# Second block of a two-block transformer: merge gate products spread over the turns of attention

## The reference, cut to what matters

```python
def hybrid_layer(x, norm_g, w_in, w_br_a, w_br_b, w_br_c, w_out, cos, sin):
    h = rmsnorm(x, norm_g)
    proj = h @ w_in                          # 1024 x 8388; m_g is its last 3072 columns
    ...
    ya = moba_attention(...)    * silu(a_g)  # 384 wide
    yb = dsa_attention(...)     * silu(b_g)  # 384 wide
    yc = dilated_mixture(...)   * silu(c_g)  # 256 wide
    gates = sigmoid(m_g).reshape(bsz, seq, 3, 1024)
    merged = (gates[:, :, 0] * (ya @ w_br_a) + gates[:, :, 1] * (yb @ w_br_b)
              + gates[:, :, 2] * (yc @ w_br_c))
    return x + merged @ w_out
```

## Time and profile before

| what | us |
|---|---|
| median of 3 runs | 1746.44 (1740.73 to 1748.66) |
| profiled execution, its time | 1738.29 |
| profiled execution, its span | 1736.5 |
| PE busy in the span | 1581.3 (91%) |
| DVE, ACT, POOL busy | 946.2, 650.5, 263.6 |
| mean granted PE clock | 0.954 of full |

### The profile page before, as it was taken

How to read it: one execution, slowest core, us unless ns; L and a number is a source line. 1 busy time by engine, 2 the same in 40 slices (tenths; PEclk the granted TensorE clock), 3 DMA queues, 4 the chain that set the end, 5 groups by cost and what they waited for, 6 DMA issues and landing times.

```text
span 1736.5 us, 23526 instructions
## 1 busy us (share of the span) xinstructions
PE 1581.3 (91%) x9394; PEld 1291.3 (74%) x9394; DVE 946.2 (54%) x1332; ACT 650.5 (37%) x947; POOL 263.6 (15%) x230
## 2 busy tenths in 40 slices
PE   4899979899999999889889996999879989997997
PEld 2774537888888887765679996789569968875996
DVE  2634443644544557624466767788426667863464
ACT  2434341521112114333443334444543444454333
POOL 0214430100000000314300001120430012125000
PEclk8999989999999999899999998999889989988999
DMA  9313781232222222319545555446105545540352
GB/s 352 97 49 122 277 233 50 72 99 98 97 97 97 97 98 73 117 43 325 137 131 191 174 192 164 144 146 195 50 14 182 182 128 177 163 146 1 115 177 98
DMA packets 168672, 234.19 MB, mean 135 GB/s; under 512 B 8929, under 2 KB 116481, under 8 KB 168449
## 3 DMA queue, kind: packets, MB, share of 16 engines
q1 hardware_dynamic: 168576, 232.86, 41.3%
HBM read 231.79 MB, written 1.05 MB: 134 GB/s over the span
## 4 chain that ended last, share of the span: by engine, by line
PE 71%; DVE 8%; ACT 5%; POOL 3%; issue 2%; DMA 1%; DVEq 0%; POOLq 0%; ACTq 0%
PE psum L615 20%; PE psum L617 19%; PE psum L616 19%; PE psum L816 3%; POOL work L1964 2%; PE psum L849 2%; DVE wl L1382 2%; PE psum L632 2%; PE psum L836 2%; PE psum L821 1%; ACT wh L1095 1%; DVE smax L1591 1%; ACT scr L1082 1%; ACT scr L1079 1%; DVE roped L1557 1%
## 5 line engine op out<-in xcount | busy, mean ns | idle before, releaser
L1382 DVE TENSOR_TENSOR wl<-raw,wh 128x2048 fp32r<-128x2048 f32 (+1 forms) x170 | 384.6, 2262 | 332.6 <-ACT wh L1095 180.2
L615 PE MATMUL psum<-hTh,wh 128*128 128x256 f32 (+1 forms) x1376 | 425.2, 309 | 10.6 <-DVE hTl L1453 6.0
L617 PE MATMUL psum<-hTh,wl 128*128 128x256 f32 (+1 forms) x1376 | 423.8, 308 | 0.0
L616 PE MATMUL psum<-hTl,wh 128*128 128x256 f32 (+1 forms) x1376 | 423.8, 308 | 0.0
L615 PEld LDWEIGHTS psum<-hTh,wh 128*128 128x128 f32 x1376 | 263.1, 191 | 26.6 <-issue 4.4
L616 PEld LDWEIGHTS psum<-hTl,wh 128*128 128x128 f32 x1376 | 263.2, 191 | 12.9
L617 PEld LDWEIGHTS psum<-hTh,wl 128*128 128x128 f32 x1376 | 263.1, 191 | 12.5
L1095 ACT ACTIVATE wh<-raw 128x2048 fp32r<-128x2048 f32 (+2 forms) x108 | 202.4, 1874 | 153.4 <-PE psum L617 142.0
L1270 ACT ACTIVATE wh<-raw 128x2048 fp32r<-128x2048 f32 x62 | 118.9, 1917 | 364.5 <-PE psum L617 364.5
L615 PE MATMUL psum<-wh,hTh 128*128 128x512 f32 (+3 forms) x576 | 221.9, 385 | 11.1 <-DVE hTl L1453 6.5
L617 PE MATMUL psum<-wh,hTl 128*128 128x512 f32 (+3 forms) x576 | 219.0, 380 | 0.0
(11 more groups left out here) (141 smaller groups left out, 1798.5 us busy)
## 6 DMA issues: line engine op xcount, KB each, us to landing
raw<-in_w_in SPq DMA_DIRECT2D x54, 1024.0 KB, 4.9
raw<-in_w_ada SPq DMA_DIRECT2D x48, 1024.0 KB, 6.4
raw<-in_w_gate SPq DMA_DIRECT2D x22, 1024.0 KB, 5.1
...
```

The costliest lines, as they stand in the source:

```text
L615: pe.matmul(o, left[0], right[0], start=first, stop=False)
L616: pe.matmul(o, left[0], right[1], start=False, stop=False)
L617: return pe.matmul(o, left[1], right[0], start=False, stop=last)
L1382: dve.tensor_tensor(wl[:, w % SPLIT, 0:m], raw[:, u % RING, 0:m], wh[:, w % SPLIT, 0:m].bitcast(F32), ALU.subtract).then_inc(lo_ready, 1)
```

## The change

The 12 gate units move from merge2 into att2. `HALF_GATES` gives each of PE's 19 turns one or two slots (after logits, after values) with 24 half-products of 24 matmuls, all accumulated in PSUM bank 7. ACT copies each finished unit raw into free SBUF (L1252 of the new kernel) and casts the next weights; the weights' remainder on DVE stands at the end of a step, the gate multiplication at its start. M stands between A and B. The sigmoids come in merge2, in place. A merge round has one weight unit, in the order A, C, B; DVE makes three products, POOL adds the first two, DVE adds the third, ACT makes hi, DVE makes lo in the next round. In merge2 PE waits for the attention outputs branch by branch.

The diff, cut to its core:

```diff
@@ -71,6 +71,9 @@
+HALF_GATES = [(1, 1) if i in (7, 8, 9, 10, 11) else (0, 1) if i == 18 else (1, 0) for i in range(19)]
+GATES_BY = [sum(map(sum, HALF_GATES[0:i + 1])) // 2 for i in range(19)]
+MERGE_BRANCHES = (0, 2, 1)
...
@@ -353,14 +362,14 @@
 
         def pairs_second():
 
-            found = []
+            found, last = [], []
             for kind in "AB":
                 for j in range(3):
                     for t in X:
                         nk = (t + 1) * P
                         mask = (t * P, nk, masks2r[:, 0, t, t * P:nk]) if kind == "A" else (0, nk, wmaskr[:, t, 0:nk])
                         at = [SV_A + HD * (2 * j + x) if kind == "A" else SV_B for x in range(2)]
-                        found.append(dict(
...
@@ -485,12 +496,13 @@
                         loads.append((raw3(u, 256)[:, 0:8, at:at + c1 - c0], kview(a["w_in_2"][l], 0, 8, c0, c1)))
                         at += c1 - c0
                     plan(loads, group_done, plan_count.next(group_done))
+            if step == "att2":
+                for n in range(12):
+                    c0 = MERGE_GATE + D * (n % 3) + 256 * (n // 3)
+                    plan([(raw3(len(units), 256), kview(a["w_in_2"][l], 0, 8, c0, c0 + 256))],
+                         group_done, plan_count.next(group_done))
             if step == "merge2":
                 for p in range(4):
-                    for br in range(3):
-                        c0 = MERGE_GATE + D * br + 256 * p
-                        plan([(raw3(len(units), 256), kview(a["w_in_2"][l], 0, 8, c0, c0 + 256))],
-                             group_done, plan_count.next(group_done))
                     loads = [(raw3(len(units), 256)[:, k0:k1, :], kview(w[l], 0, k1 - k0, 256 * p, 256 * p + 256))
                              for w, k0, k1 in ((a["w_br_a_2"], 0, 3), (a["w_br_b_2"], 3, 6), (a["w_br_c_2"], 6, 8))]
                     plan(loads, group_done, plan_count.next(group_done, 3))
@@ -714,19 +726,20 @@
                 if later:
                     later.pop()()
 
-            def narrow(u, k0, k1, rhs, free):
-
-                b = WIDE[pj[0] % 5]
-                pj[0] += 1
+            def narrow(u, k0, k1, rhs, free, at=None, halves=(0, 1)):
+
+                b = WIDE[pj[0] % 5] if at is None else at
+                pj[0] += at is None
                 o = bank(b)
                 hi, lo = parts(split_of[u], 256)
-                for f in range(2):
+                for f in halves:
                     for k in range(k0, k1):
                         mm = product(o[:, SEQ * f:SEQ * f + SEQ],
                                      (hi[:, k, P * f:P * f + P], lo[:, k, P * f:P * f + P]), rhs(k),
                                      k == k0, k == k1 - 1)
-                mm.then_inc(group_done, 1)
-                freed[b] = (free, c.next(free))
+                if halves[-1] == 1:
+                    mm.then_inc(group_done, 1)
+                    freed[b] = (free, c.next(free))
 
             def wide(u, groups, w, free, between=None, ring=WIDE, fresh=False):
 
@@ -851,21 +864,33 @@
                     if 0 <= i - 3 < len(steps):
                         values(steps[i - 3])
-                    if beside:
-                        next(beside, None)
+                    next(beside, None)
+
+            def merge_gates():
+
+                n = 0
+                for slots in HALF_GATES:
+                    for half in slots:
+                        if half:
+                            if n % 2 == 0:
+                                have_parts(unit[0])
+                            narrow(unit[0], 0, KC, lambda k: (hTh[:, k, 0:SEQ], hTl[:, k, 0:SEQ]), evac_act,
+                                   BESIDE, (n % 2,))
+                            unit[0] += n % 2
+                            n += 1
+                        yield
 
             def fourier_beside(l):
 
@@ -1039,20 +1065,20 @@
-                    pe.wait_ge(evac_act, c.now(evac_act))
-                    attention(att[step, l], OUT2)
+                    pe.wait_ge(evac_act, ready2[0])
+                    attention(att[step, l], True, merge_gates())
                 if step == "wout1":
                     pe.wait_ge(mix_split, pairs_until("att1", l))
                     pe.wait_ge(mixT_ready, c.now(mixT_ready))
                     wout(tiles_of(l), lambda n, t: mixT(n, P * t, P * t + P, False))
                 if step == "merge2":
-                    pe.wait_ge(mix_split, pairs_until("att2", l))
                     pj[0] = 0
                     for p in range(4):
-                        for br in range(3):
-                            gate_groups()
                         have_parts(unit[0])
-                        for k0, k1 in ((0, 3), (3, 6), (6, 8)):
+                        for br in MERGE_BRANCHES:
+                            k0, k1 = ((0, 3), (3, 6), (6, 8))[br]
+                            if p == 0:
+                                pe.wait_ge(mix_split, pairs_until("att2", l) - (5, 0, 3)[br])
                             narrow(unit[0], k0, k1, lambda k: mixT(k, 0, SEQ, True), evac_dve)
                         unit[0] += 1
                 if step == "wout2":
@@ -1220,6 +1247,13 @@
                         lead(i - behind)
                     if i < n_four:
                         four_led(i)
+                    if second and GATES_BY[min(i, 18)] - (i == 18) > gate:
+                        act.wait_ge(group_done, c.next(group_done))
+                        act.activation(mgate[gate], ps[BESIDE], ACT.Copy).then_inc(evac_act, 1)
+                        gate += 1
+                        n_used[0] += 1
+                    if second:
+                        split_ahead()
 
             def four_evacuated():
 
@@ -1255,6 +1289,12 @@
                                                      scale=scl[:, l, which, k, s:s + 1])
                             ins.then_inc(hTh_ready, 1)
                 split_ahead()
+
+            def lead_merged(p):
+
+                act.wait_ge(merged_sum, c.next(merged_sum))
+                act.activation(mmh[:, 2 * p:2 * p + 2, :], branch[:, p % 2, 2, :].rearrange("p (k n) -> p k n", k=2),
+                               ACT.Copy).then_inc(merged_lead, 1)
 
             def ffn(l):
                 nt = len(tiles_of(l))
@@ -1330,22 +1370,19 @@
                         n_used[0] += 1
                         split_ahead(1 if k == 3 else 2)
                 if step == "att2":
-                    attention(att[step, l], splits_beside(step, l), True)
+                    attention(att[step, l], {}, True)
                 if step == "merge2":
-                    pj[0] = 0
-                    act.wait_ge(pv_done, att["att2", l][-1]["step"] + 1)
                     for p in range(4):
-                        for k in range(3):
-                            if p >= 2 and k == 0:
-                                act.wait_ge(merged_ready, 4 * l + p - 1)
-                            evac_group(mgate[:, p % 2, k, :], (0, 512), ACT.Sigmoid, ring=WIDE)
-                            n_used[0] += 1
-                            split_ahead()
-                        pj[0] += 3
+                        for br in MERGE_BRANCHES:
+                            g = mgate[3 * p + br]
+                            act.activation(g, g, ACT.Sigmoid).then_inc(sigmoid_ready, 1)
                         c.next(group_done, 3)
                         c.next(evac_dve, 3)
                         n_used[0] += 1
+                        if p:
+                            lead_merged(p - 1)
                         split_ahead()
+                    lead_merged(3)
                 if step == "ffn":
                     ffn(l)
                     for t in tiles_of(l):
@@ -1613,38 +1650,45 @@
+                        gate(i - 4)
                     if i < n:
                         shifts(i)
                     if beside:
                         next(beside, None)
                     if 0 <= i - 1 < n:
                         shares(i - 1)
-                    if second:
-                        if 0 <= i - 4 < n:
-                            gate(i - 4)
-                        if 0 <= i - 5 < n:
-                            keep_mixed(i - 5)
-                    elif 0 <= i - 4 < n:
-                        keep_mixed(i - 4)
+                    at = i - (5 if second else 4)
+                    if 0 <= at < n:
+                        keep_mixed(at)
                     if beside:
                         next(beside, None)
                     if i in splits_at:
                         ahead, lift = splits_at[i]
                         passed[0] += lift
                         split_ahead(ahead)
+                    if second:
+                        while gates_split < GATES_BY[min(max(i - 1, 0), 18)]:
+                            gates_split += 1
+                            n_used[0] += 1
+                            c.next(group_done)
+                            c.next(evac_act)
```

(52 more changed lines are left out.)

55 lines of the change are left out of this document (34 added, 21 removed).

## The result

The changed kernel takes 1715.95 us (median of 4 runs, 1713.48 to 1716.63), the one before 1744.48 in the same comparison (4 runs, 1740.73 to 1748.66). The ratio is 0.9839, 95% interval 0.9809 to 0.9868: faster, by 28.5 us where 13.2 had been forecast. The profiled execution took 1716.63 us, with a span of 1714.8 where the one before had 1736.5.

The account below looks back on a forecast made before the run. A five-engine chain bounds att2 while PE fills merge2. Joined, PE's 136.9 plus 17.6 of waits make 154.5 against 162.6 us; less 1.5 for clock, 13.2 gained in all: 1725.1 profiled, 1733 median, range 1711 to 1748.

Parts of the forecast that it names:

- PE's own work: PE's products in a layer's joined att2 and merge2 stage, all at full clock: 136.9 us.
- Waits: PE's waiting that stays in a layer's joined stage, summed turn by turn: 17.6 us.
- M turns: Attention turns of the wide M pairs: PE waits 10.6 us a layer, mostly for ACT's copy behind exponentials.
- logits(7): M-turn logits in att2, waiting for exponentials that start after turn 6's transposes: 1.3 us.
- plain turns: Attention turns of pairs A and B: PE waits 2.85 us a layer together, 1.1 of it in turn 2.
- A merge round: DVE's cycle from sum to sum in merge2: 6.95 us, 1.1 more than PE's.
- Rivals C and D: C: POOL's sum sets merge2, 1739, chance 0.1. D: bank 7 bounds, copies behind ACT's cast, 1756, chance 0.1.
- The clock: One short fall of PE's clock in the M turns: 1.5 us a layer taken off the gain.
- 162.6 us per layer: Time before the change from att2's preceding work to the last weights' product; less 136.9, 25.7 us of possible gain.
- the median of the runs stands 8.15 above it: Offset from profiled execution to median of runs, added at the end: 1725.1 becomes 1733.
- Rival B: Clock falls in the M turns, leaving about 8 us of PE's work undone per layer: 1746, no change; chance 0.13.
- Rival A: Waits mostly hidden: half of them and no clock loss, 17 us a layer gained, 1712; chance 0.2.

Follow-up runs that it names:

- evac_first: Kernel after, with ACT copying a finished gate unit from bank 7 earlier: ahead of transposes' copies in M turns, otherwise ahead of `lead`; 1701.35 us, ratio 0.9741.
- before_again: The kernel before, unchanged, run more often; medians 1742.56 us (17 runs) and 1746.97 us (12 runs), profiled execution 1737.73 us.
- before_fill: Kernel before, with six extra unused 128x256 products in each turn of att2 and both gated outputs sharing one bank; 1744.69 us, ratio 1.0017.
- spread_only: Kernel after, with merge sums, hi and lo all on DVE as before the change; 1726.35 us, ratio 0.9902.
- m_last: Kernel after, with M last (order A, B, M), double slots moved with it, branches in order A, B, C; 1720.36 us, ratio 0.9862.
- evac_twice: Kernel after, with ACT's copy of bank 7 done twice for each gate unit; 1734.62 us, ratio 0.9953.
- last_lo_first: evac_first, with DVE also making the last attention chunk's lo ahead of the last weight remainder; 1688.67 us, ratio 0.9699.
- pool_sums: last_lo_first, with POOL making both sums of a merge round; 1690.25 us, ratio 0.9689.

## Why the prediction was right in kind and wrong in size

- PE's own work, 136.9: measured 135.4 (evac_first, clock 1.00). 1.5 too much.
- Waits, 17.6: measured 15.5, and at the places and with the sizes listed. M turns were forecast at 10.6 with logits(7) and came to 9.96; merge2 1.95, came 1.62; wout2 2.2, came 1.59; plain turns 2.85, came 2.31, with turn 2 at 1.40 where 1.1 was forecast.
- A merge round, 6.95: measured 6.33. From the end of the second product to DVE's last sum the forecast had lo 0.7, POOL's sum 1.65 and a handover 0.2, 2.55 one after the other; the rows have 1.99, because POOL's sum begins beside the lo and takes 1.80 there. Rivals C and D did not occur: POOL's sum never took more than 1.81, and no unit's copy was held up by a cast.
- The clock, 1.5 taken off: measured 3.2 us of busy time above 135.4, in the M turns as was said, but twice the size.
- The stage: 154.5 and 1.5 for the clock, 156.0, against 154.2 and 153.9. That 154.5 itself stands so near is luck: it has no clock loss in it, and 1.5 too much work and 2.1 too much waiting fill the place of the 3.2.

**The step that failed is the stage before, "162.6 us per layer", read off one execution and taken as waits alone, and with it "the median of the runs stands 8.15 above it".** The prediction read 162.6 - 136.9 = 25.7 as waiting that could be saved, and the clock only as something that could be lost. The rows to see more were there: att2's clock of 0.80, products of the earlier trace rows at full clock beside a stretch at 0.53. Of the 25.7, 16.8 was idle time and 8.9 was PE's products at half clock. The change removed hardly any idle time (1.2) and most of the second part (7.2). And this second part is not the same in each execution: before_again has 3.1 us more of it in each layer. The first layer of eight runs, us:

| run | idle | clock | length x (1 - clock) | PE busy above 135.4 |
|---|---|---|---|---|
| before | 16.8 | 0.92 | 13.0 | 10.4 |
| before_again | 17.0 | 0.90 | 16.6 | 13.4 |
| before_fill, less 13.7 | 12.8 | 0.97 | 5.0 | 4.9 |
| spread_only | 16.9 | 0.98 | 3.1 | 3.5 |
| m_last | 14.9 | 0.96 | 6.3 | 6.0 |
| after | 15.6 | 0.98 | 3.1 | 3.2 |
| evac_twice | 21.2 | 0.95 | 8.2 | 7.4 |
| evac_first | 7.4 | 1.00 | 0 | 0 |

The last two columns go together, so what PE's busy time holds above 135.4 follows the clock; before and before_again, one program, show it without any change in how the work is cut up. Where the fourth column is the larger one, a part of the low clock lies over idle time. Rival B ("the clock falls") priced only a loss; falls came, of 3.2 us a layer, but the kernel before had 10.4 to 13.4 of them.

What the terms come to. The two stages brought 3.8 us more than forecast in the profiled pair. Taken from before_again they bring 23.6 in place of 17.0, 6.6 more. For the stretches behind a stage the forecast had nothing: 2.5 us between the stages and 0.7 behind the second, 3.2, which hang on the clock behind a gap and were not settled. Together 13.2 + 3.8 + 6.6 + 3.2 = 26.8, against 28.5 measured with an interval of 23 to 33; the rest is within it. That the runs of before had stages like before_again's rather than like the first execution's is an estimate from two traces; with the first one's the sum is 20.2, outside the interval. The 8.15 added at the end is no part of this sum: no run shows a fixed distance between a profiled execution and the median, which went from 9.2 below it (before_again) to 5.8 above it (evac_twice); the stretch ahead of att2, which no change here touches, alone differs by up to 10.7 us.

That the loss by clock is a part of what a wait costs was then measured: 1.4 a microsecond taken away, 1.7 added. The Trainium skill (TensorE: Matmul & The Clock Gate, Part 1) speaks of a monitor that passes fewer pulses when the engine has been less busy. The runs agree where only waits change: idle time of 7.4, 15.6 and 21.2 us in the same stage goes with a clock of 1.00, 0.98 and 0.95. But the sum of the waits alone does not settle it: 16.8 and 16.9 us go with 0.92 (before) and 0.98 (spread_only).

Rival A's number, 1712, is nearer than the forecast's 1733, but not its premise: 15.5 of the 17.6 us of waiting stayed. Halving the waits is possible, and evac_first does it (7.4 us).

**The better version.** last_lo_first, 1688.67 us, is 3.0% under the kernel before (ratio 0.9699) and ahead of the kernel after: the bank's copy earlier in ACT's order, and the last lo ahead of the last remainder. pool_sums equals it. The copy of turn 2, 1.40 us of wait a layer, is still open in both.
